# Three feed-forward blocks: gate and up products in Strassen's form, down product in pieces between the pairs

## What is computed

```python
def swiglu(x, w_gate, w_up, w_down):
    return (jax.nn.silu(x @ w_gate) * (x @ w_up)) @ w_down
...
    for layer in range(DEPTH):
        x = x + FFN_RESIDUAL * swiglu(rms_norm(x, g[0]), ...)
        ...   # even layer: dilated attention and pooling; odd layer: mLSTM
        x = x + FFN_RESIDUAL * swiglu(rms_norm(x, g[2]), ...)
```

## Time and profile before

| | us |
|---|---|
| median of three runs (2052.86 to 2054.8) | 2054.67 |
| the profiled execution | 2058.72 |
| its span | 2056.9 |
| TensorE busy | 2028.6 |
| VectorE / ScalarE / GpSimd busy | 893.5 / 726.9 / 457.7 |

### The profile page before, as it was taken

How to read it: one execution, slowest core, us unless ns; L and a number is a source line. 1 busy time by engine, 2 the same in 40 slices (tenths; PEclk the granted TensorE clock), 3 DMA queues, 4 the chain that set the end, 5 groups by cost and what they waited for, 6 DMA issues and landing times.

```text
span 2056.9 us, 23014 instructions
## 1 busy us (share of the span) xinstructions
PE 2028.6 (99%) x9098; PEld 1642.8 (80%) x9098; DVE 893.5 (43%) x1068; ACT 726.9 (35%) x990; POOL 457.7 (22%) x358
## 2 busy tenths in 40 slices
PE   8999999999999999999999999999998999999999
PEld 6888888876778888888888888877776788888887
DVE  5333333544543333344333334783467743333332
ACT  5323223425532232243223223554545333223231
POOL 1202111142322020122202012354033512112021
PEclk9999999999999999999999999999998999999999
DMA  5333333421233333333333333322200233333333
GB/s 175 94 101 93 102 92 130 147 82 42 63 91 103 92 100 94 98 97 108 101 94 97 98 95 100 93 82 82 72 1 1 72 103 93 94 101 93 102 92 103
DMA packets 55729, 188.91 MB, mean 92 GB/s; under 512 B 6096, under 2 KB 6352, under 8 KB 55632
## 3 DMA queue, kind: packets, MB, share of 16 engines
q1 hardware_dynamic: 55632, 187.52, 29.9%
HBM read 182.78 MB, written 4.72 MB: 91 GB/s over the span
## 4 chain that ended last, share of the span: by engine, by line
PE 94%; DVE 2%; ACT 1%; POOL 1%; DMA 1%; issue 1%; SPq 0%; DVEq 0%; POOLq 0%; ACTq 0%
PE PS L435 28%; PE PS L437 28%; PE PS L436 28%; PE PS L768 2%; PE PS L751 1%; PE PS L594 1%; DVE SQ L1341 1%; DMA RAW<-gu_dram 1%; PE PS L657 1%; PE PS L557 1%; PE PS L596 1%; PE PS L595 1%; PE PS L639 0%; DVE LO L1124 0%; POOL SQ L1460 0%
## 5 line engine op out<-in xcount | busy, mean ns | idle before, releaser
L1124 DVE TENSOR_TENSOR LO<-RAW,HI 128x1024 fp32r<-128x1024 f32 (+1 forms) x336 | 419.8, 1249 | 1009.6 <-ACT HI L830 1009.5
L435 PE MATMUL PS<-XH,HI 128*128 128x512 f32 x1792 | 702.8, 392 | 11.6 <-DVE XL L1132 11.5
L436 PE MATMUL PS<-XL,HI 128*128 128x512 f32 x1792 | 698.6, 390 | 0.0
L437 PE MATMUL PS<-XH,LO 128*128 128x512 f32 x1792 | 698.3, 390 | 0.0
L830 ACT ACTIVATE HI<-RAW 128x1024 fp32r<-128x1024 f32 (+1 forms) x344 | 357.1, 1038 | 694.6 <-DMA RAW<-gu_dram 368.9
L435 PEld LDWEIGHTS PS<-XH,HI 128*128 128x128 f32 x1792 | 337.1, 188 | 88.9 <-DVE LO L1124 10.8
L436 PEld LDWEIGHTS PS<-XL,HI 128*128 128x128 f32 x1792 | 337.1, 188 | 70.7 <-issue 1.4
L437 PEld LDWEIGHTS PS<-XH,LO 128*128 128x128 f32 x1792 | 337.1, 188 | 70.6
L1470 POOL TENSOR_TENSOR TMP<-TMP,RSTD 128x512 f32<-128x512 f32 x88 | 113.4, 1289 | 741.0 <-ACT TMP L862 741.0
L437 PE MATMUL PS<-HH,LO 128*128 128x512 f32 x704 | 273.9, 389 | 0.0
L435 PE MATMUL PS<-HH,HI 128*128 128x512 f32 x704 | 273.9, 389 | 0.0
(11 more groups left out here) (189 smaller groups left out, 1501.6 us busy)
## 6 DMA issues: line engine op xcount, KB each, us to landing
RAW<-gu_dram SPq DMA_DIRECT2D x176, 512.0 KB, 3.6
RAW<-down_dram SPq DMA_DIRECT2D x64, 512.0 KB, 3.6
RAW<-oin_dram SPq DMA_DIRECT2D x32, 512.0 KB, 3.6
RAW<-down_dram SPq DMA_DIRECT2D x32, 384.0 KB, 3.0
RAW<-ein_dram SPq DMA_DIRECT2D x16, 512.0 KB, 3.6
RAW<-oout_dram SPq DMA_DIRECT2D x16, 512.0 KB, 3.6
RAW<-eout_dram SPq DMA_DIRECT2D x8, 512.0 KB, 3.6
skew_dram<-STG SPq DMA_DIRECT2D x1, 2560.0 KB, 9.6
```

Source lines behind the costliest of these rows:

```text
L435: pe.matmul(PS[bank][:], HI[j][:, c], hi(k), start=(n == 0), stop=False)
L436: pe.matmul(PS[bank][:], HI[j][:, c], lo(k), start=False, stop=False)
L437: last = pe.matmul(PS[bank][:], LO[j][:, c], hi(k), start=False, stop=(n == len(order) - 1))
L1124: dve.tensor_tensor(LO[j][:, 0:kt * P], RAW[j][:, 0:kt * P], HI[j][:, 0:kt * P].bitcast(F32), ALU.subtract).then_inc(lo_ready, 1)
```

## The change

Feed-forward blocks 1, 2 and 3 (not 0) get a new routine, `block_ffn`. Its first three pairs (`PLAIN`) are as before. In the other 19 the 1024 input features and the 512 tokens are halved, and gate and up form the two output halves of a 2 x 2 block product. Strassen's form (Winograd's variant) makes it from seven products instead of eight, each of 4 k-tiles and 256 tokens: 7 x 4 x 3 = 84 matmuls of 256 columns a pair, where there were 48 of 512.

What it takes for that: four sums of token blocks (`BFR`, once a feed-forward block, made beside the plain pairs, `form` on VectorE, split in `form_split`), four sums of weight blocks a pair (`ASR`, `sums_first` to `sums_third` on VectorE, split into `ASH` on ScalarE and `ASL` on VectorE), and after the products five additions through `MID` (`copy_one`, `mid_two`, `mid_five`, `mid_three`, `whole_up`, `whole_gate`) that leave gate and up in their banks, gate negated. HI and LO of gate's left half are no longer made.

The down product of hidden tiles 0 to 15 is cut into 16 pieces, one behind each of pairs 4 to 19 (`early`): 4 hidden tiles into two output tiles, 24 matmuls of 512 columns, with weights loaded into `DRAW` in the TMP region and added to `X` at once (`early_add`). Tiles 16 to 21 follow at the end as before; the first two output tiles leave the last hidden tile for later. The loops over thirds are gone from these three blocks, and the load of `WGR` moves behind block 2's loads. GpSimd does the same two operations a pair, in place in `GT`.

```diff
-Q_FFN = (0, 23, 40, 69)
+Q_FFN = (0, 23, 36, 61)
 Q_EIN, Q_EOUT = 17, 21
-Q_OIN, Q_OOUT = 57, 65
-Q_END = 86
+Q_OIN, Q_OOUT = 49, 57
+Q_END = 74
+
+PLAIN = 3
+BLOCKS = FT - PLAIN
+EARLY = 16
...
+                for n in range(SLOTS, NU):
+                    u = n if n < 2 * PLAIN else n ^ 1
+                    load(q0 + n // 4, n % 4, gu_d[f, u])
+                    p = n // 2 - 1
+                    if n % 2 and has_early(p):
+                        load_early(p)
+                for m in range(KX):
...
+                def product(out, w_hi, w_lo, tokens):
+                    x_hi, x_lo = tokens
+                    for k in range(4):
+                        c = slice(k * P, k * P + P)
+                        pe.matmul(out, w_hi[:, c], x_hi(k), start=(k == 0), stop=False)
+                        pe.matmul(out, w_hi[:, c], x_lo(k), start=False, stop=False)
+                        last = pe.matmul(out, w_lo[:, c], x_hi(k), start=False, stop=(k == 3))
+                    return last
...
+                def block(p):
+                    n, g = base + 2 * p, block_count(f, p)
+                    up, gate = 2 * (p % 2), 2 * (p % 2) + 1
+                    up_bank, gate_bank = (PS[i] for i in block_banks(p))
+                    left, right = slice(0, 4 * P), slice(4 * P, 8 * P)
+                    low, high = slice(0, TH_), slice(TH_, T)
+                    pe.wait_ge(lo_ready, n + 1)
+                    pe.wait_ge(bank_free, n + 2)
+                    if p == PLAIN:
+                        pe.wait_ge(std_ready, r + 1)
+                        pe.wait_ge(form_lo, 4 * f)
+                    if g:
+                        pe.wait_ge(mid_made, 5 * g - 2)
+                    product(PS[4][:, low], HI[up][:, left], LO[up][:, left], plain(0, 0)).then_inc(one_done, 1)
+                    pe.wait_ge(sum_lo, 2 * g + 2)
+                    product(PS[5][:, low], *summed(p, 2), form(2)).then_inc(six_done, 1)
+                    product(gate_bank[:, high], *summed(p, 1), form(0)).then_inc(five_done, 1)
+                    pe.wait_ge(one_copied, g + 1)
+                    product(PS[4][:, low], *summed(p, 0), form(1)).then_inc(seven_done, 1)
+                    product(up_bank[:, low], HI[up][:, right], LO[up][:, right], plain(4, 0)).then_inc(unit_done, 1)
+                    product(up_bank[:, high], *summed(p, 3), plain(4, 1)).then_inc(three_done, 1)
+                    pe.wait_ge(mid_made, 5 * g + 2)
+                    pe.wait_ge(lo_ready, n + 2)
+                    product(gate_bank[:, low], HI[gate][:, right], LO[gate][:, right], form(3)).then_inc(unit_done, 1)
+
+                def early(p):
+                    e, c = early_count(f, p), (p - 4) // 4
+                    pe.wait_ge(early_lo, e + 1)
+                    pe.wait_ge(hl_ready, 22 * f + 4 * c + 4)
+                    for half in range(2):
+                        if e:
+                            pe.wait_ge(early_free, 2 * e - 1 + half)
+                        for k in range(4):
+                            col = slice((4 * half + k) * P, (4 * half + k) * P + P)
+                            h = (4 * c + k) % 8
...
+                    unit(q0 + n // 4, n % 4, KX, xh, xl)
+                for p in range(PLAIN, FT):
+                    block(p)
+                    if has_early(p):
+                        early(p)
+                for n0, n1 in ((0, 5), (5, 6)):
+                    for m in range(2):
...
+                def form_inputs(a):
+                    gain = C_NORM + 8 * (2, 3, 5)[f - 1]
+                    if a:
+                        act.wait_ge(form_made, 4 * (f - 1) + a)
+                    act.activation(MID[:, 0, :], X[:, a, TH_:T], ACT.Copy, scale=par(gain + a))
+                    act.activation(MID[:, 2:4, :], X[:, 4 + a, :].rearrange("p (h t) -> p h t", h=2), ACT.Copy,
+                                   scale=par(gain + 4 + a)).then_inc(form_in, 1)
...
+                def copy_one(p):
+                    g = block_count(f, p)
+                    act.wait_ge(one_done, g + 1)
+                    if g:
+                        act.wait_ge(mid_made, 5 * g - 1)
+                    act.activation(MID[:, 0, :], PS[4][:, 0:TH_], ACT.Copy).then_inc(one_copied, 1)
+
+                whole, right = slice(0, KMAX * P), slice(4 * P, KMAX * P)
+                for n in range(2 * PLAIN):
+                    p = n // 2
+                    if n % 2:
+                        h_high(p)
+                    else:
+                        silu(p, 1.0)
+                    if n + 4 < 2 * PLAIN:
+                        split(n + 4, whole)
+                    if n < 4:
+                        form_inputs(n)
+                    if 1 <= n <= 4:
+                        form_split(n - 1)
+                    if n == 4:
+                        split(6, whole)
+                        split(7, right)
+                        sums_split(PLAIN, 0)
+                        sums_split(PLAIN, 1)
+                for p in range(PLAIN, FT):
+                    nxt = p + 1 if p + 1 < FT else None
+                    copy_one(p)
+                    if p > PLAIN and not has_early(p - 1):
+                        h_high(p - 1)
+                    if nxt:
+                        split(2 * nxt, whole)
+                        split(2 * nxt + 1, right)
+                        sums_split(nxt, 0)
+                        sums_split(nxt, 1)
+                    else:
+                        split(NU, slice(0, 6 * P))
+                        split(NU + 1, slice(0, 6 * P))
+                    if has_early(p):
+                        act.wait_ge(early_in, 16 * (early_count(f, p) + 1))
+                        act.activation(DHI[:], DRAW[:], ACT.Copy).then_inc(early_hi, 1)
+                    silu(p, -1.0)
+                    if has_early(p):
+                        h_high(p)
+                split(NU + 2, slice(0, 6 * P))
+                h_high(FT - 1)
+                split(NU + 3, slice(0, 6 * P))
+                for m in range(KX):
+                    if after:
+                        residual_tile(q0 + (NU + m) // 4, m % 4, r, m)
+                    if m < 4:
+                        split(NU + 4 + m, slice(0, 6 * P))
+                    elif after:
+                        split(NU + 4 + m, whole)
...
+                def form(a):
+                    gain, done = C_NORM + 8 * (2, 3, 5)[f - 1], 4 * (f - 1) + a
+                    dve.wait_ge(form_in, done + 1)
+                    dve.scalar_tensor_tensor(BFR[:, a, 0, :], X[:, a, 0:TH_], par(gain + a), MID[:, 0, :], ALU.mult,
+                                             ALU.subtract).then_inc(form_step, 1)
+                    dve.tensor_tensor(BFR[:, a, 1, :], MID[:, 3, :], MID[:, 0, :], ALU.subtract)
+                    dve.wait_ge(form_step, 2 * done + 1)
+                    dve.scalar_tensor_tensor(BFR[:, a, 2, :], BFR[:, a, 0, :], -1.0, MID[:, 3, :], ALU.mult,
+                                             ALU.subtract).then_inc(form_step, 1)
+                    dve.wait_ge(form_step, 2 * done + 2)
+                    dve.scalar_tensor_tensor(BFR[:, a, 3, :], BFR[:, a, 2, :], -1.0, MID[:, 2, :], ALU.mult,
+                                             ALU.subtract).then_inc(form_made, 1)
...
+                def sums_first(p):
+                    b, q = p % 2, (base + 2 * p) // 4
+                    dve.wait_ge(weights_in[2 * b], 16 * (q + 1))
+                    dve.wait_ge(weights_in[2 * b + 1], 16 * (q + 1))
+                    gate = RAW[2 * b + 1]
+                    other = PAIR[b][:].rearrange("p (t c) -> p t c", c=4 * P)[:, 0:6:5, :]
+                    dve.tensor_tensor(ASR[:, b, 0:2, :], other, gate[:, 0:4 * P].unsqueeze(1).to_broadcast([P, 2, 4 * P]),
+                                      ALU.add).then_inc(sum_made, 1)
...
+                def whole_gate(p):
+                    g = block_count(f, p)
+                    bank = halves(PS[block_banks(p)[1]])
+                    dve.wait_ge(mid_made, 5 * g + 3)
+                    dve.wait_ge(unit_done, base + 2 * p + 2)
+                    dve.tensor_tensor(bank, bank, MID[:, 3, :].unsqueeze(1).to_broadcast([P, 2, TH_]),
+                                      ALU.add).then_inc(mid_made, 1)
+
+                def early_split(p):
+                    dve.wait_ge(early_hi, early_count(f, p) + 1)
+                    dve.tensor_tensor(DLO[:], DRAW[:], DHI[:].bitcast(F32), ALU.subtract).then_inc(early_lo, 1)
+
+                def early_add(p, half):
+                    e, m = early_count(f, p), 2 * ((p - 4) % 4) + half
+                    dve.wait_ge(early_done if half else early_half, e + 1)
+                    dve.scalar_tensor_tensor(X[:, m, :], PS[6 + half][:], 0.5, X[:, m, :], ALU.mult,
+                                             ALU.add).then_inc(early_free, 1)
...
+                for n in range(2 * PLAIN):
+                    if n % 2:
+                        up(n // 2)
```

(69 more changed lines are left out.)

217 lines of the change are left out of this document (198 added, 19 removed).

## The result

The changed kernel took 2064.61 us, median of six runs (2063.26 to 2067.28), against 2054.74 us for the kernel before (six runs beside it, 2052.44 to 2059.23): ratio 1.0046, 95% interval 1.0032 to 1.0059. It is slower by 9.9 us. I had forecast 2052.5, with a chance of 0.34 for slower; the time lies within the range (2042 to 2068), near its upper end, and that is luck: no rival of mine is the reason. The profiled execution took 2063.33 us, its span 2061.5.

What follows compares the result with a forecast made beforehand. TensorE, busy 99% of the span, was taken as the bound. Per block 17.9 us gained against 17.2 us of waits and clock, net -0.7, -2.1 in all; from the median 2054.67, 2052.5 us, range 2042 to 2068.

Steps and rivals of the forecast that it cites:

- 5. HL of pair 21 for the last two down tiles: 0.4 us: Block's end: TensorE waits 0.4 us a block for pair 21's HL, needed by the last two down tiles.
- gain of 19 pairs: Gate/up pairs in the new form: 10.88 us becomes 9.94 each, 17.9 us a block, 53.8 in all.
- first down piece: At pair 4: VectorE, late from pair 3, needs 10.7 us against six products' 8.6; TensorE waits 2.0 us a block.
- HL, restarts: Per block: 0.4 us waiting for pair 21's HL, plus five restarts of TensorE after waits at 0.09, 0.5 us.
- The price of a product of 256 columns: New-form pairs: 118.3 ns a product, range 117.5 to 119.5, from twelve starts in 1.42 us; pays below 129.5.
- The first wait: Before each block's first Strassen pair: sums and weight split ready at 41.7 us, TensorE at 34.1; wait 7.6 us.
- The clock: Behind each block's first wait: granted clock at half for 6.2 us, 3.1 us lost a block.
- The short waits: TensorE waits on VectorE: 1.8 us at the second Strassen pair, 2.0 at pair 4's down piece, 1.8 at pair 21.
- Rival C: Pairs with a down piece: VectorE becomes the bound, +0.3 us a pair, 2067 us; chance 0.13.
- Rival B: Clock also falls at the short waits, 3.2 us a fall, +4.1 a block: 2065 us; chance 0.17.
- Rival D: A product is never shorter than its weight load, 0.181 us: +246 us, 2299; chance 0.02 together with the rest.
- the exclusion: GpSimd and VectorE operations block each other: 0.7 us a pair; without it and half the clock loss, waits total 12.5.

Runs made afterwards that it cites:

- the filler: The changed kernel with 24 added products of 512 columns, result unread, before each block's first Strassen pair: 2064.09 us, ratio 1.0039 to the kernel before.

## Why the prediction was wrong

The sign was wrong for one term that is not in the sum. The walk through the queues ended with each block's last product, and one block's sum was taken three times, as if the stage behind it started no later. At "5. HL of pair 21 for the last two down tiles: 0.4 us" it had what TensorE loses to the late HL, and that is right (0.34 us). What VectorE loses to it, a first residual 2.8 us later, was not followed, although the loop of 4.12 to 4.40 us against 4.08 is in the trace of before and never makes it up. That loop pays it out at the next stage's first tiles: 2.9 us, twice, and 1.7 us of clock each. With the order of that loop changed the kernel is level with the kernel before (1.0001). The down product was put down as "only reordered"; it was, but what waits for it was moved.

Inside the block the net was near, by errors that cancel. Third block, from the starts of its products in the trace:

| term | forecast us | measured us |
|---|---|---|
| gain of 19 pairs | 17.9 | 14.9 |
| first Strassen pair's wait | 7.6 | 6.8 |
| clock behind it | 3.1 | 1.5 |
| pair 4, second product | 1.8 | 1.9 |
| first down piece | 2.0 | 1.7 |
| pair 21 | 1.8 | 1.9 |
| HL, restarts | 0.9 | 0.6 (restarts are in the rows above) |
| net | -0.7 | -0.5 (by the stage -0.4) |

**The price of a product of 256 columns** was the largest error inside the block. The period of a pair with its down piece, first product to first product:

```profile
1800.85 0.28 PE L580 MATMUL BANKS<-XH,HI 128*128 128x256 f32 x1
1800.96 0.28 PE L581 MATMUL BANKS<-XL,HI 128*128 128x256 f32 x1
...
1816.39 0.28 PE L580 MATMUL BANKS<-XH,HI 128*128 128x256 f32 x1
```

15.54 us, the same to 0.01 in thirteen periods in a row, where 15.38 was forecast: 10.07 for the 84 products and 5.47 for the down piece. 10.07 / 84 = 119.9 ns, not the 118.3 of the earlier trace rows, and outside my 117.5 to 119.5. 1.6 ns seem nothing, but 4788 products make 7.7 us of them. I took the price from twelve starts in 1.42 us, where a hundredth of a microsecond at each end is 1.7 ns; my bounds were narrower than what the row could tell. Rounding is not all of it: to the nanosecond the same twelve starts take 118.4 ns each in the trace before and 119.2 in the one after, so a stretch as short as this is good to 0.8 ns at best. Whether the rest of the difference lies in the place or in the weights is open.

**The first wait**: the chain is the one walked (gate, SiLU, splits, forms); in the third block it ended 40.3 us after the block's start where 41.7 was walked, TensorE was there 0.6 us sooner, and the wait was 0.8 us shorter. In the second block it was 5.20, because the wait at its start had put off the later products as well (7.30 once that wait was gone).

**The clock**: 3.0, 1.5 and 1.5 us lost in the three blocks, not 3.1 each, and the filler showed that taking the loss away gains next to nothing, since the next split is late too. So this term was no cost of its own here: an input that came late stood behind it.

**The short waits** in pairs 4 and 21 came as walked.

**Rival C** (VectorE as the bound of the paired stretch) is out: no wait there.

**Rival B** is out: the clock held behind each of the short waits of 1.4 to 1.6 us. What brought 2065 was a wait of another length at another place.

**Rival D** is out: 119.9 ns stand in a stream with a weight load at each product. Its 2299 was also summed from the wrong base: the 246 us are counted from pairs of 10.88 us, but added to a time that has the gain of 53.8 in it, so it should have been about 2352.

Two readings of the walk were loose. In the earlier trace rows split and GpSimd operation overlap for 0.39 us and the split is 0.24 longer, so it did not stand to the end of the other; at the overlap of 1.25 us above the same 0.15 us is missing. The shown terms of the exclusion add up to 1.6 us a block, and no run shows the 3.1 that leaving it out was said to give. And the earlier trace rows has no GpSimd operation beside the one from PSUM; what shows it is the residual at 926.22 above.

## What to carry to other kernels

Follow an edit's lateness past the edited code, on every engine, until a loop with slack absorbs it: a loop in which two engines take turns, and which is a few per cent slower than the engine it feeds, absorbed nothing here, and passed it on to the next stage. Where a new form needs a preparation that is longer than the work ahead of it, one more unit in the old form is the cheapest cover (0.8 us of gain given up, 8.8 us a block won on balance). And a price that is multiplied by thousands is to be read over a stretch of hundreds, not a dozen.
